# A hybrid attention layer: reloads of the mixed tiles issued by ScalarE, their stores by GpSimd, SP's DMA queue left to weights and input

## What is computed

```python
h = rmsnorm(x); proj = h @ w_in             # split in gated linear attention and differential attention
o_gla  = head_rmsnorm(gla_chunked(gq, gk, gv, g)) * silu(ggate)        # 4 heads of 128: columns 0..511
o_diff = head_rmsnorm(diff_attention(q, k, dv, lam)) * silu(dgate)     # 4 heads of 128: columns 512..1023
mixed = concatenate([o_gla, o_diff], axis=-1)
x = x + mixed @ w_out
x = x + cross_attention(rmsnorm(x), rmsnorm(mem), w_cq, w_ckv, w_co)
return rmsnorm(x)
```

## Time and profile before

| | us |
|---|---|
| median of 3 timed runs | 870.24 (870.15 to 870.57) |
| profiled execution | 874.1 |
| its span, by the profile | 872.4 |
| TensorE busy | 850.4 (97%) |
| VectorE, ScalarE, GpSimd busy | 529.6, 397.2, 44.1 |
| granted clock of TensorE, mean | 0.996 |
| tile_a from mixed | 16 DMAs of 256 KB |
| mixed from mix_out | 16 DMAs of 128 KB, 32 of 64 KB |

### The profile page before, as it was taken

The page is one execution under the profiler, slowest core; times in us unless marked ns, Lnnn a source line. Parts: engine busy times, 40 slices in busy tenths (PEclk is TensorE's granted clock), DMA queues, the critical chain, the costliest instruction groups (busy, mean ns, idle before and its releaser), DMA issues.

```text
span 872.4 us, 12997 instructions
## 1 busy us (share of the span) xinstructions
PE 850.4 (97%) x4676; PEld 705.0 (81%) x4676; DVE 529.6 (61%) x1274; ACT 397.2 (46%) x982; POOL 44.1 (5%) x84
## 2 busy tenths in 40 slices
PE   7999999999999999999999899999999999999997
PEld 6777877777788888888878887888888888888885
DVE  6667667767578668678768765223336654355543
ACT  7765444444346345445545655203425543234422
POOL 2000000000000000000000000000100000010001
PEclk9999999999999999999999999999999999999999
DMA  8321112112212112102112266521022202351112
GB/s 270 110 78 37 31 41 69 37 43 67 59 31 55 35 34 56 34 22 67 43 63 74 88 213 216 184 86 61 32 89 74 68 29 73 97 192 49 49 49 97
DMA packets 53592, 67.69 MB, mean 78 GB/s; under 512 B 5844, under 2 KB 32536, under 8 KB 53528
## 3 DMA queue, kind: packets, MB, share of 16 engines
q1 hardware_dynamic: 53528, 66.85, 24.2%
HBM read 58.44 MB, written 8.39 MB: 77 GB/s over the span
## 4 chain that ended last, share of the span: by engine, by line
PE 78%; DVE 11%; ACT 4%; issue 3%; DMA 3%; POOL 0%; SPq 0%; POOLq 0%; ACTq 0%
PE bank L1350 12%; PE bank L1352 12%; PE bank L1351 12%; PE banks2to L1350 8%; PE banks2to L1352 8%; PE banks2to L1351 8%; PE banks6to L1401 4%; PE banks2to L1573 4%; PE bank L1599 2%; DVE w_lo L1004 2%; DVE state L1183 1%; ACT junk L789 1%; ACT w_hi L793 1%; DMA tile_a<-mixed 1%; DVE mix_out L1207 1%
## 5 line engine op out<-in xcount | busy, mean ns | idle before, releaser
L1350 PE MATMUL bank<-w_hi,actT_hi 128*128 128x512 f32 x472 | 189.8, 402 | 1.2 <-DVE gate L1161 0.3
L1352 PE MATMUL bank<-w_hi,actT_lo 128*128 128x512 f32 x472 | 184.5, 391 | 0.0
L1351 PE MATMUL bank<-w_lo,actT_hi 128*128 128x512 f32 x472 | 184.3, 390 | 0.0
L1004 DVE SCALAR_TENSOR_TENSOR w_lo<-w_raw,vecs,w_hi 128x512 fp32r<-128x512 f32 x120 | 86.6, 747 | 43.5 <-ACT w_hi L793 43.5
L1350 PEld LDWEIGHTS bank<-w_hi,actT_hi 128*128 128x128 f32 x472 | 88.9, 188 | 22.2 <-DVE gate L1161 3.5
L1352 PEld LDWEIGHTS bank<-w_hi,actT_lo 128*128 128x128 f32 x472 | 88.6, 188 | 19.2
L1351 PEld LDWEIGHTS bank<-w_lo,actT_hi 128*128 128x128 f32 x472 | 88.9, 188 | 16.6
L793 ACT ACTIVATE w_hi<-w_raw,vecs 128x512 fp32r<-128x512 f32 x120 | 82.4, 717 | 11.8 <-DMA w_raw<-in_w_cq 6.1
L1350 PE MATMUL banks2to<-w_hi,actT_hi 128*128 128x512 f32 x168 | 66.5, 396 | 0.0
L1352 PE MATMUL banks2to<-w_hi,actT_lo 128*128 128x512 f32 x168 | 65.6, 390 | 0.0
L1351 PE MATMUL banks2to<-w_lo,actT_hi 128*128 128x512 f32 x168 | 65.5, 390 | 0.0
(11 more groups left out here) (288 smaller groups left out, 1818.9 us busy)
## 6 DMA issues: line engine op xcount, KB each, us to landing
w_raw<-in_w_in SPq DMA_DIRECT2D x56, 256.0 KB, 2.9
w_raw<-in_w_ckv SPq DMA_DIRECT2D x32, 256.0 KB, 3.4
w_raw<-in_w_cq SPq DMA_DIRECT2D x32, 256.0 KB, 2.8
w_raw<-in_w_co SPq DMA_DIRECT2D x32, 256.0 KB, 2.7
stage_in<-in_x SPq DMA_DIRECT2D x8, 512.0 KB, 4.9
tile_a<-mixed SPq DMA_DIRECT2D x16, 256.0 KB, 3.6
w_raw<-in_w_out SPq DMA_DIRECT2D x16, 256.0 KB, 3.1
x_res<-in_x SPq DMA_DIRECT2D x8, 512.0 KB, 4.9
```

Source lines behind the costliest of these rows:

```text
L1004: return dve.scalar_tensor_tensor(dst, src, scale, hi.bitcast(F32), ALU.mult, ALU.subtract)
L1350: pe.matmul(dst, l_hi, r_hi, start=start, stop=False)
L1351: pe.matmul(dst, l_hi, r_lo, start=False, stop=False)
L1352: return pe.matmul(dst, l_lo, r_hi, start=False, stop=stop)
```

## The change

The three branches ofin, pvfin and loadm leave SP's program. GpSimd's program gets ofin and pvfin, with the same waits and the same DMAs, at the same places of the list. ScalarE's program gets loadm, likewise with its waits on the transposes of two tiles earlier and on the stores. Nothing else changes: the list, the buffers, the semaphores and the sizes are the same.

```diff
@@ SP's program (sync)
-                elif kind == "ofin":
-                    s = w[0]
-                    p, t = divmod(s, TT)
-                    sp.wait_ge(of_dve, at("ofin", s))
-                    sp.dma_start(mixed[cols(t), 256 * p:256 * p + 256],
-                                 mix_out[:, 256 * (s % 2):256 * (s % 2) + 256]).then_inc(d_mixg[s % 2], 16)
-                elif kind == "pvfin":
...
-                elif kind == "loadm":
...
@@ GpSimd's program
+                elif kind == "ofin":
+                    s = w[0]
+                    p, t = divmod(s, TT)
+                    pool.wait_ge(of_dve, at("ofin", s))
+                    pool.dma_start(mixed[cols(t), 256 * p:256 * p + 256],
+                                 mix_out[:, 256 * (s % 2):256 * (s % 2) + 256]).then_inc(d_mixg[s % 2], 16)
+                elif kind == "pvfin":
+                    i = w[0]
+                    h, t = divmod(i, TT)
+                    pool.wait_ge(pf_dve, at("pvfin", i))
+                    pool.dma_start(mixed[cols(t), GH * GDV + P * h:GH * GDV + P * h + P],
+                                 mix_out[:, P * (i % 4):P * (i % 4) + P]).then_inc(d_mixd[i % 4], 16)
@@ ScalarE's program
+                elif kind == "loadm":
+                    t, kk = w
+                    n = RELOAD[("MT", t, kk)]
+                    if n >= 2:
+                        act.wait_ge(ring_pe, TR[RELOADS[n - 2]] + 1)
+                    if kk == 0:
+                        for j in range(2):
+                            act.wait_ge(d_mixg[j], 16 * GLA_STEPS // 2)
+                    else:
+                        i = DIFF_STEPS - TT + t
+                        act.wait_ge(d_mixd[i % 4], 16 * (i // 4 + 1))
+                    act.dma_start(tile_a[:, 512 * (n % 2):512 * (n % 2) + 512],
+                                 mixed[cols(t), 512 * kk:512 * kk + 512]).then_inc(d_tile[n % 2], 16)
```

## The result

The changed kernel takes 873.61 us (median of 7 runs, 872.09 to 874.89) where the kernel before takes 870.24 us (7 runs, 869.77 to 871.51). The medians are 3.4 us apart. The ratio of the runs is 1.0034, with a 95% interval of 1.0023 to 1.0046, which is 3.0 us, between 2.0 and 4.0: slower. The forecast was 872.4 us, slower, in a range of 868.4 to 875.4.

The account below looks back on a forecast made before the run. TensorE, busy 97% of the span, was taken as the bound, so only its waits count; 870.24 + 4.7 (new stall with clock loss) - 2.5 (fill gain in a timed run) = 872.4 us, range 868.4 to 875.4.

Parts of the forecast that it names:

- ScalarE's wait at the first two reloads: Ahead of E 0, near 223 us: E 0 3.2 us late, TensorE standing about 3.0 us at S 1.
- the move of E 0 with the store still on SP: If ScalarE issues the first two reloads as SP did, E 0 moves from 223.88 to 226.37, by 2.5 us.
- What GpSimd's store adds: Delay of E 0 because the awaited store comes from GpSimd: between 0 and 1.1 us, taken as 0.7 us.
- the bounds of 0.34 and 1.4 us: How long one store holds GpSimd: at least SP's 0.34 us issue, at most twice the longest rs_o, 1.4 us.
- The clock behind the new stop: Behind TensorE's stall at S 1: 1.7 us lost to a lower clock, with about 70% confidence.
- The stores on GpSimd: Stores moved from SP to GpSimd: removing 48 issues from SP worth nothing, cost of 47 stores zero.
- The fourteen issues in ScalarE's gaps: The other fourteen reloads on ScalarE, in the attention steps: issues of 0.32 to 0.4 us fall in gaps, cost zero.
- The gain in the fill: Between 500 and 531 us, reloads issued earlier: 4.2 us gained in the profiled execution, 2.5 us in a timed run.
- the largest: TensorE's reload wait until 530.49 in the fill: 1.86 us and 1.7 us of clock loss, both to go.
- the 3.9 us between the profiled time and the median: Profiled 874.1 us against timed 870.24 us: part probably the transfer waits and clock loss the change can give back.
- rival A: Slower still: fill gain at most 0.5 us in timed runs, stall with clock loss paid fully, 874.4 us; chance 0.18.
- the first reload: Fill reload issued at 504.55, no longer behind three weights: between -0.3 and +0.85 us, taken as 0.4 us gained.

Follow-up runs that it names:

- the ordinary execution of before: The kernel before, unedited, profiled and timed again: span 868.4 us in the profile, median 870.24 us, ratio 0.9998.
- filling the stop: The changed kernel with twenty useless identity transposes on TensorE ahead of the second scores (S 1): 872.27 us, ratio 1.0017 to the kernel before.

## Why the prediction was right, and where its sizes were off

**ScalarE's wait at the first two reloads.** Right in mechanism, place and chain: E 0 released by a store, qkT_lo late, TensorE standing at S 1, and undoing these two alone takes the loss away. The size was 2.6 us instead of 3.0 us. Of the two terms, the one that was too large is mainly the move of E 0 with the store still on SP: taken as 2.5 us from the times of SP's reloads, it was 2.2 us (E 0 began 225.36 - 221.98 = 3.38 us behind the start of mix_out with the reloads alone moved, and 223.10 - 221.92 = 1.18 us behind it in the ordinary execution of before), since ScalarE issued them 1.88 us behind the store and SP had done so only after 2.23 us. What GpSimd's store adds, taken as 0.7 us, was 0.6 us (stops of 2.6 and 2.0 us). That this was so near is partly luck, because the 0.7 us was the length of an rs_o and stood for the issue alone; the trace has 0.27 us of later issue and 0.35 us of later landing. GpSimd was held 0.58 us, between the bounds of 0.34 and 1.4 us. The 2.3 us that the Trainium skill (DMA: Bandwidth & Descriptors, section Anatomy of one DMA — SWDGE (gpsimd) path) gives for such a DMA was close to the landing of 2.2 us here.

**The clock behind the new stop.** Expected with 70%, 1.7 us. It fell in two profiled executions of three that had the stop (the changed kernel and the one with the reloads alone), by 1.7 us of work in both, and filling the stop brought 1.3 us or somewhat more in the median. In TensorE's timeline the fall at 230 cost 1.5 us: from the second scores to the last map's wait the changed kernel took 495.82 - 229.50 = 266.3 us, and the execution without the fall there 494.34 - 229.53 = 264.8 us.

**The stores on GpSimd.** Zero, as predicted: 870.30 us against 870.29.

**The fourteen issues in ScalarE's gaps.** Zero, as predicted: the issue took 0.33 us, and with them 869.54 us is under the kernel before.

**The gain in the fill.** Here the sum failed. Of 2.5 us taken for a timed run, 0.75 us came with the first two reloads on SP, and 1.1 us with all sixteen on ScalarE and those two later in the list, each against the kernel before in its own batch. Two steps were off. First, the waits were read from one execution, and the size of the largest, with its clock loss, was that execution's own: 1.86 + 1.7 us there, 0.81 + 0 in an ordinary one. The prediction saw the 3.9 us between the profiled time and the median and put part of it down to these waits; it should have put nearly all of this gain there, as rival A did. Second, the first reload was taken to win 0.4 us by no longer queueing behind three weights. It won nothing: it was issued at 508.02, which is 504.55 plus the 3.5 us by which TensorE was late there, because the operation ahead of it in ScalarE's queue waits for VectorE:

```profile
507.87 0.31 ACT L776 ACTIVATE junk<-pv_f 128x128 bf16<-128x128 f32 x1 [1.28 <-DVE pv_f L1266]
508.02 0.33 ACTq L976 DMA_DIRECT2D tile_a<-mixed  x1
```

It landed 5.1 us after its issue, as it had in SP's queue (5.0). The rule of the Trainium skill (DMA: Bandwidth & Descriptors, section Rules for kernel authors), that a second queue brings no bandwidth, agrees with that.

The sum also has a slip: with the first reload between -0.3 and +0.85 us, the gain in the profiled execution has its low end at 3.5 us, not at the 2.9 us that was written.

With the sizes found: 870.24 + 2.6 + 1.3 - 0.75 = 873.4 us, against 873.61 measured. So two terms were too large on opposite sides: the stop with its clock loss by 0.8 us (3.9 instead of 4.7) and the gain by 1.75 us. They partly cancel, and that the time fell only 1.2 us beside the forecast is luck to that extent; the direction is not, since it follows from the stop. The kernel came out between the forecast and rival A, which came nearer in its condition, a small gain (0.5 us at most; it was 0.75) with the stop paid (4.7 us; it was 3.9).

## What to carry to other kernels

A DMA issued from a computing engine's queue takes its waits with it: before moving one, look at what stands behind it in that queue and at how much later its semaphore comes, here 2.2 us of store landing ahead of a step with 0.2 us of cover. Where a transfer is late, ask first what it is queued behind; moving four reloads ahead of weights in SP's queue brought 2.2 us, and the second and third queue nothing beyond it. And where a profiled execution is slower than every timed run, take a second profile before its largest wait is counted as a gain.

## What the runs showed of the hardware

- A stop of TensorE is followed by some 3.4 us at the 1.2 GHz level in some executions and not in others: stops of 2.6 us were seen with and without it, stops of 1.2 us likewise, and stops of 1.86 and 2.0 us with it. By the granted clock it was 1.7 us of work each time. In TensorE's timeline it cost 1.5 us behind the second scores, 1.6 us behind the wait at 530 of the kernel before (335.5 us from there to the last matmul instead of 333.9), and nothing where later waits took it up. The runs of the changed kernel spread from 872.09 to 874.89 us, with the stop filled from 871.55 to 872.91 us.
- Twenty useless transposes in the stop kept the clock at 2.4 GHz in the profiled execution and made the kernel 1.3 us faster in the median.
- The last 128 KB store held GpSimd for 0.58 us and landed after 2.2 us (2.1 in the median of sixteen), on SP 0.34 and 1.8 us. A 256 KB reload took 0.33 us to issue on ScalarE and 0.38 us on SP, both medians of sixteen.
